# Two-layer hybrid decoder trunk on one core: paired 64-row scores, X^T by transposition, and moved steps where the mix and the MLP groups end

## What is computed

```python
h = rms_norm(x, ln_mix_pre)
(a_q, a_k, a_v, i_q, i_k, i_w, b_q, b_k, b_v, b_a, b_b, b_z,
 c_q, c_k, c_v, c_g, gate_logits) = split_projection(h @ w_in)
# A: scores = sum_h relu(iq_h . ik) * w_h; keep the 128 best causal keys of each query;
#    attention of 4 heads of 128 over them
# B: conv + SiLU on q/k/v, delta rule in chunks, T = inverse(I + M), gated
# C: retention, 4 heads with keys of 64, fixed decay, gated
merged = g0 * (y_a @ w_ba) + g1 * (y_b @ w_bb) + g2 * (y_c @ w_bc)
x = x + rms_norm(merged @ w_out, ln_mix_post)
ff = jnp.square(jax.nn.relu(rms_norm(x, ln_mlp_pre) @ w_up)) @ w_down
x = x + rms_norm(ff, ln_mlp_post)
```

## Time and profile before

| | |
|---|---|
| time of the runs | 1983.54 us median, 1982.48 to 1984.13 |
| profiled execution | 1989.03 us, span 1987.2 us |
| mean granted TensorE clock | 0.989 |
| busy share of the span | TensorE 97%, weight loads 78%, VectorE 58%, ScalarE 24%, POOL 18% |
| chain that ended last | TensorE 91%, ScalarE 4%, VectorE 3%, issue 2% |

### The profile page before, as it was taken

How to read it: one execution, slowest core, us unless ns; L and a number is a source line. 1 busy time by engine, 2 the same in 40 slices (tenths; PEclk the granted TensorE clock), 3 DMA queues, 4 the chain that set the end, 5 groups by cost and what they waited for, 6 DMA issues and landing times.

```text
span 1987.2 us, 25235 instructions
## 1 busy us (share of the span) xinstructions
PE 1932.3 (97%) x8926; PEld 1556.1 (78%) x8926; DVE 1145.5 (58%) x1958; ACT 470.2 (24%) x919; POOL 348.7 (18%) x549
## 2 busy tenths in 40 slices
PE   8999999999999999999999999999999999999998
PEld 7867667879878888788878667678888788887887
DVE  6855688854464642454477557888434655424534
ACT  3153343211333100011122533523122331000111
POOL 2211111110120222222112111111101102221220
PEclk9999999999999999999999999999999999999999
DMA  6432112321430422222222321222215213332221
GB/s 233 138 117 70 64 59 88 90 75 56 178 117 1 145 98 96 85 95 95 85 85 97 116 69 64 69 79 89 79 49 214 73 44 116 99 101 83 99 96 53
DMA packets 72478, 186.79 MB, mean 94 GB/s; under 512 B 18304, under 2 KB 30784, under 8 KB 71488
## 3 DMA queue, kind: packets, MB, share of 16 engines
q1 hardware_dynamic: 41328, 152.10, 22.7%
q10 hardware_dynamic: 31056, 33.38, 5.0%
HBM read 174.40 MB, written 11.06 MB: 93 GB/s over the span
## 4 chain that ended last, share of the span: by engine, by line
PE 91%; ACT 4%; DVE 3%; issue 2%; POOL 0%; DMA 0%; ACTq 0%; SPq 0%; POOLq 0%; DVEq 0%
PE psD L1043 23%; PE psD L1045 22%; PE psD L1044 22%; PE psM L1043 4%; PE psM L1045 4%; PE psM L1044 4%; PE psM L1102 2%; PE psM L1109 1%; PE psM L1305 1%; PE psM L1199 1%; PE psM L1207 1%; PE psM L1323 1%; PE psM L1311 1%; ACT wide L1543 1%; PE psM L1116 1%
## 5 line engine op out<-in xcount | busy, mean ns | idle before, releaser
L1043 PE MATMUL psD<-a_hi,w_hi 128*128 128x512 f32 (+2 forms) x1488 | 601.4, 404 | 14.2 <-DVE wide L2272 6.6
L1045 PE MATMUL psD<-a_hi,w_lo 128*128 128x512 f32 (+2 forms) x1488 | 578.9, 389 | 0.0
L1044 PE MATMUL psD<-a_lo,w_hi 128*128 128x512 f32 (+2 forms) x1488 | 578.3, 389 | 0.0
L953 DVE TENSOR_TENSOR w_lo<-raw,w_hi 128x1024 fp32r<-128x1024 f32 x208 | 255.4, 1230 | 306.5 <-POOL w_hi L1021 305.7
L1043 PEld LDWEIGHTS psD<-a_hi,w_hi 128*128 128x128 f32 (+1 forms) x1488 | 281.8, 189 | 96.0 <-issue 32.2
L1020 POOL TENSOR_TENSOR w_hi<-raw,tabs 128x1 fp32r<-128x1 f32 x272 | 60.8, 223 | 1599.8 <-PE psD L1045 1376.8
L1045 PEld LDWEIGHTS psD<-a_hi,w_lo 128*128 128x128 f32 (+1 forms) x1488 | 281.4, 189 | 58.9 <-issue 0.3
L1044 PEld LDWEIGHTS psD<-a_lo,w_hi 128*128 128x128 f32 (+1 forms) x1488 | 281.9, 189 | 58.2 <-issue 4.5
L1021 POOL TENSOR_SCALAR w_hi<-raw 128x1023 fp32r<-128x1023 f32 x272 | 296.8, 1091 | 0.0
L1801 ACT CAST f_hi<-gt 128x512 f32 x64 | 40.0, 624 | 487.4 <-DVE gt L2244 487.4
L2241 DVE TENSOR_SCALAR gt<-psD 128x512 f32<-128x512 f32 x64 | 44.3, 691 | 140.2 <-PE psD L1045 140.2
(11 more groups left out here) (269 smaller groups left out, 2620.2 us busy)
## 6 DMA issues: line engine op xcount, KB each, us to landing
raw<-in_ws SPq DMA_DIRECT2D x272, 512.0 KB, 3.3
s_raw<-in_wo ACTq DMA_DIRECT2D x14, 512.0 KB, 11.1
out<-x SPq DMA_DIRECT2D x8, 512.0 KB, 5.1
x<-rows_d ACTq DMA_DIRECT2D x4, 1024.0 KB, 5.7
x<-out ACTq DMA_DIRECT2D x2, 2048.0 KB, 8.4
e_raw<-in_wo ACTq DMA_DIRECT2D x8, 512.0 KB, 6.5
tabs<-in_tab SPq DMA_DIRECT2D x1, 2944.0 KB, 12.2
x<-in_x SPq DMA_DIRECT2D x4, 512.0 KB, 6.6
```

What stands on the lines that cost most here:

```text
L953: dve.tensor_tensor(w_lo[:, s, :], raw[:, s, :], w_hi[:, s, :].bitcast(F32), ALU.subtract) \
L1043: pe.matmul(out, lhi, rhi, start=start, stop=False)
L1044: pe.matmul(out, lhi, rlo, start=False, stop=False)
L1045: return pe.matmul(out, llo, rhi, start=False, stop=stop)
```

## The change

Seven edits, all in the lists of steps and in the steps themselves; the computation stays.
1. `rs(a, m)` and `index(tb, a)` issue two matmuls one behind the other, on partitions 0 to 63 and 64 to 127, into two banks. The steps on VectorE and ScalarE stay per head. In the planner, the ring of three banks becomes a choice of the banks that are free first. Retention takes two heads at a time, so the second head's output accumulates in one of the three small banks.
2. `xt` at levels 4 and 5 turns the new X; ScalarE copies it to X^T. Level 6 stays a product, subtracted on VectorE.
3. The probabilities are scaled on ScalarE, and the reciprocal stays on VectorE.
4. In the prefix `rot 4` comes behind the units 6 and 7. The w_lo of the planned region's second slab is issued with the prefix, not by the planner. The planner's starting times change.
5. In the tail the stays come earlier, each with a semaphore of its own for its load. `lo_merged` for 0 to 3 comes before merge 2's slab, for 4 and 5 before merge 3's. ScalarE's table load comes behind the last a_hi. The first token tile takes the staying slabs in another order.
6. x1 is turned among the slabs of the tiles 2 and 3, and the splits move with it.
7. At the end of a group the last `lo_slab` comes after `add_half1`.

```diff
+TURNS = {(2, 2): 0, (2, 5): 1, (3, 5): 2}
@@ schedule
     for r in range(4):
-        prefix.append(("rot", r + 1))
-        if r == 3:
+        if r < 3:
+            prefix.append(("rot", r + 1))
+        else:
             prefix += [("piece", j, "cv", 0) for j in range(PIECES - 1)] + [("cv", 0)]
         for j in (2 * r, 2 * r + 1):
             prefix.append(("unit", j))
...
+        if r == 3:
+            prefix.append(("rot", 4))
         prefix.append(("turn", r))
...
+    def paired(w):
+        return .207 + .213 * w
...
-            op("pe", "xt", n, l, t=.9, to=("dve", "XT", n, l), after=[("act", "left", n, l), ("dve", "XT", n, l - 1), ("pe", "xx", n, l)])
-            op("dve", "XT", n, l, t=read(2, 1.2), after=[("pe", "xt", n, l), ("dve", "X", n, l)])
+                op("pe", "xt", n, l, t=.44, to=("act", "XT", n, l), after=[("dve", "X", n, l)])
+                op("act", "XT", n, l, t=copied(), after=[("pe", "xt", n, l)])
+            else:
+                op("pe", "xt", n, l, t=.9, to=("dve", "XT", n, l), after=[("act", "left", n, l), ("act", "XT", n, l - 1)])
+                op("dve", "XT", n, l, t=read(2, 1.2), after=[("pe", "xt", n, l)])
...
-            op("dve", "prob", tb, h, t=.2 + read(w, slow), after=[("act", "sexp", tb, h), ("dve", "smax", tb, H - 1)])
+            op("dve", "rinv", tb, h, t=.2, after=[("act", "sexp", tb, h)])
+            op("act", "prob", tb, h, t=copied(w), after=[("dve", "rinv", tb, h)])
...
-    free = {"pe": 0.0, "act": 9.0, "dve": 11.0}
+    free = {"pe": 0.0, "act": 4.0, "dve": 5.0}
...
-    rounded(slabs + 2, 0.0)
-    first_slab = slabs_before = slabs + 1
+    first_slab = slabs_before = slabs + 2
...
+    def emptied(bank):
+        return end.get(user[bank], 1e9) if user[bank] else 0.0
+
+    def ring(n):
+        return sorted(range(3), key=emptied)[:len(drain[n])]
...
+        if n == ("pe", "vn", 0):
+            at = max(at, 2.5)
         if n in drain:
-            at = max(at, drained([drain[u] for u in small[-3:-2]]) + latency if len(small) >= 3 else 0)
+            at = max(at, emptied(ring(n)[-1]) + latency)
...
-    tail += [("mgate", "B", 3), ("merge", "B", 0), ("mgate", "B", 4), ("mgate", "B", 5), ("merge", "B", 1), stays[0],
-             ("mgate", "B", 6), stays[1], ("mgate", "B", 7), stays[2], ("merge", "B", 2), *stays[3:5], ("merge", "B", 3), *stays[5:]]
+    tail += [("mgate", "B", 3), ("merge", "B", 0), ("mgate", "B", 4), ("mgate", "B", 5), stays[0], ("merge", "B", 1), *stays[1:3],
+             ("mgate", "B", 6), *stays[3:5], ("mgate", "B", 7), *stays[5:], ("merge", "B", 2), ("merge", "B", 3)]
...
     opened = every(prefix, 0)
-    opened.remove(("dve", "lo", slabs_before + 1))
@@ TensorE
-                    def index(tb, i):
+                    def index(tb, a):
+
                         pe.wait_ge(*on("rot_done", 9))
-                        hp = slice(64 * (i % 2), 64 * (i % 2) + 64)
-                        ps = small_bank(("il", tb, i))
-                        small_done(pe.matmul(ps[:, 0:(tb + 1) * P], iq[hp, i // 2, cut(tb)],
-                                             ik[hp, 0:(tb + 1) * P], start=True, stop=True))
+                        banks = [small_bank(("il", tb, 2 * a + i)) for i in range(2)]
+                        for i, ps in enumerate(banks):
+                            hp = slice(64 * i, 64 * i + 64)
+                            small_done(pe.matmul(ps[:, 0:(tb + 1) * P], iq[hp, a, cut(tb)],
+                                                 ik[hp, 0:(tb + 1) * P], start=True, stop=True))
...
                     def xt(n, l):
-                        if l == FIRST:
-                            pe.wait_ge(*on(f"xi_in{n % 2}", 32 * (n // 2 + 1)))
-                        right("xt", n, l)
+                        if l == LEVELS - 1:
+                            right("xt", n, l)
+                        else:
+                            for s, v in drained(("xx", n, l)):
+                                pe.wait_ge(*on(s, v))
+                            turn_heads(("xt", n, l), lambda h: B["X", n % 2][:, cut(h)])
...
-                        for j, (_, k, ks, c, _) in enumerate(STAYING):
+                        for j in (0, 1, 3, 4, 5, 2, 6) if t == 0 else range(len(STAYING)):
+                            _, k, ks, c, _ = STAYING[j]
+                            if (t, j) in TURNS:
+                                turn_x1(TURNS[t, j])
...
-                    for t in range(READY):
+                    for t in range(ST):
                         out_tile(t)
-                    for t in range(READY - 1):
-                        turn_x1(t)
-                    out_tile(ST - 1)
-                    turn_x1(READY - 1)
@@ ScalarE
                     def left(n, l):
                         if l > FIRST:
-                            mid(act, ("xt", n, l - 1))
+                            mid(act, ("xx", n, l - 1))
...
+                    def turned(n, l):
+                        sig(act.copy(B["XT", n % 2], mid(act, ("xt", n, l))[:, :]), f"XT{n % 2}")
...
+                    def prob(tb, h):
+                        w = slice(0, (tb + 1) * P)
+                        act.wait_ge(*on("rinv", H * tb + h + 1))
+                        sig(act.activation(pr[:, h, w], pr[:, h, w], ACT.Copy, scale=rinv[:, h:h + 1]), "prob")
...
                     def stay(j):
-                        if j == 0:
-                            act.wait_ge(*on("stay_in", 16 * len(STAYING)))
+                        act.wait_ge(*on(f"stay_in{j}", 16))
...
                     slab(act, ("mgate", "B", KT - 1))
-                    act.preload_act_table_set("natural_log_exp_and_others")
                     for k in range(KT):
                         act.wait_ge(*on("merged", KT + k + 1))
                         sig(act.mul(a_hi[:, k, :], wt[:, k, :], 0.5), "a_hi")
+                    act.preload_act_table_set("natural_log_exp_and_others")
...
-                        if t == READY - 1:
-                            for i in range(READY - 1):
-                                hi_x1(i)
+                        for i in {1: (0, 1), 2: (2,)}.get(t, ()):
+                            hi_x1(i)
@@ VectorE
-                        if b and j == 3:
-
-                            for k in range(KT - 2):
+                        if b and j >= 2:
+
+                            for k in (range(4), range(4, 6))[j - 2]:
                                 lo_merged(k)
...
-                        if t == READY:
-                            lo_x1(READY - 1)
                         diagonal("pre_mlp", t)
-                        if t == READY - 1:
-                            for i in range(READY - 1):
-                                lo_x1(i)
+                        for i in {1: (0, 1), 2: (2,)}.get(t, ()):
+                            lo_x1(i)
...
                         add_half0(g)
-                        lo_down(g, range(FG // 2, FG))
+                        lo_down(g, range(FG // 2, FG - 1))
                         for t in range(ST):
                             add_half1(g, t)
+                        lo_down(g, [FG - 1])
```

More of the change, by code:

```diff
@@ L253, in schedule @@
     op("act", "cv", 3, t=ST * copied(), after=[("pe", "cv", 3)])
[L255 to L267, removed]
+    for i in range(ST * H // 2 + 1):
+        if i < ST * H // 2:
+            a, m = divmod(i, ST)
+            pair = range(2 * a, 2 * a + 2)
+            past = [("pe", "rv", 2 * ((i - 2) // ST) + 1, (i - 2) % ST)] if i >= 2 else []
+            op("pe", "rs", a, m, t=paired(ST - m), to=[("dve", "rp", h, m) for h in pair], after=[("act", "cv", 3)] + past)
+            for h in pair:
+                freed = ("pe", "rv", h, m - 1) if m else ("pe", "rv", h - 2, ST - 1)
+                op("dve", "rp", h, m, t=read(ST - m), after=[("pe", "rs", a, m), freed])
+        if i:
+            a, m = divmod(i - 1, ST)
+            for h in range(2 * a, 2 * a + 2):
+                op("pe", "rv", h, m, t=column(ST - m), to=("act", "ret", h) if h % 2 and m == 0 else None,
+                   after=[("dve", "rp", h, m), ("act", "cv", 3)])
+                if m == ST - 1:
+                    op("act", "ret", h, t=copied(), after=[("pe", "rv", h, m)])
     order = None
@@ L296, in schedule @@
                 ring = [("dve", "index", (q - 2) // IH + 1, (q - 2) % IH)] if q >= 2 else [("pe", "rv", H - 1, ST - 1)]
-                op("pe", "index", tb, i, t=column(w), to=("act", "index", tb, i), after=[("dve", "turn", 8)] + ring)
-                op("act", "index", tb, i, t=copied(w), after=[("pe", "index", tb, i)] + ring)
+                if i % 2 == 0:
+                    op("pe", "index", tb, i // 2, t=paired(w), to=[("act", "index", tb, i), ("act", "index", tb, i + 1)],
+                       after=[("dve", "turn", 8)] + ring)
+                op("act", "index", tb, i, t=copied(w), after=[("pe", "index", tb, i // 2)] + ring)
                 op("dve", "index", tb, i, t=read(w, slow) + (.3 if i == IH - 1 else 0),
```

(23 more changed lines are left out.)

62 lines of the change are left out of this document (28 added, 34 removed).

## The result

The changed kernel takes 1934.8 us (median of four executions, 1933.2 to 1942.1) against 1983.8 of the kernel before: a ratio of 0.9758, 95% interval 0.9742 to 0.9775, or 48 us less. The profiled execution took 1936.0 with a span of 1934.2, 53.0 less than the span of the profiled one before.

What follows compares the result with a forecast made beforehand. TensorE bounds the kernel, busy in 97% of the span, with its waits and low clock behind some. 16.5 + 7.4 + 9.1 + 6.8 + 8.9 + 11.3 - 6 = 54.0 off 1983.5 gives 1929.5 us, range 1918 to 1950.

Steps and rivals of the forecast that it cites:

- pairs: rs and index steps between dense matmuls: fewer 64-row detours on TensorE save 14.7 to 18.1 us, taken as 16.5.
- X^T: Levels 4 and 5: transposing instead of products saves 0.46 us on each of 16 steps, 7.4 us; dense pieces cover the chain.
- probabilities: Scaling moved to ScalarE: no gain taken, as TensorE never waits for the removed line; some 5 us possible loss.
- prefix: Waits for the last unit and a w_lo, plus low clock behind: 9.1 us gained, between 5 and 11.7.
- out slabs: Waits for a_lo going into the out slabs, plus clock: 6.8 us gained (4 to 8), w_lo then late by 0.65.
- x1: Turning among the out slabs lets the up slabs start 2.76 us earlier per layer; with clock 8.9, lower end 5.
- groups: Between the groups: TensorE's 3.3 us wait per layer and the low clock go, 11.3 us gained (10 to 12).
- new waits: Between 176 and 500, pairs ask for two small banks at once: three more waits per layer, 6 us lost.
- the list does not fit (1): Rival: slightly wrong planner durations cause many waits between 176 and 500; gain 20 to 32, time 1951 to 1963, chance 0.10.
- turning lowers the clock (2): Rival: clock falls to 1.2 GHz around each of 16 more turnings, costing 27 to 48: 1957 to 1978, chance 0.02.
- Pairs without overlap (3): Rival: the second matmul's bank is held until the first is over, losing all 16.5: 1946 us, chance 0.03.
- Waits of 1.5 us at each pair (4): Rival: TensorE waits for a second bank at all 40 detours; slower from 1.5 us each, 1997 at twice 0.93, chance 0.04.

Runs made afterwards that it cites:

- e5: Changed kernel with X^T at levels 4 and 5 computed again by four products and a subtraction on VectorE: 1935.4 us, ratio 0.9749.
- e12: The kernel of e11 with X^T at levels 4 and 5 by products and a subtraction on VectorE again: 1926.1 us, ratio 0.9709.
- e1: Changed kernel with the last w_lo of a group put back ahead of the four adds: 1948.7 us, ratio 0.9823.
- e2: Changed kernel with x1 turned behind the tiles again instead of among the slabs, splits included: 1942.3 us, ratio 0.9798.
- e3: Changed kernel with the old tail: late stays, one semaphore, old merge order, table load and first-tile order: 1943.9 us, ratio 0.9801.
- e6: Changed kernel with the old prefix end: rot 4 before the last units, later w_lo, old planner starting times: 1946.5 us, ratio 0.9816.
- e9: Changed kernel with its list of steps kept, but probabilities scaled on VectorE at the reciprocal's place: 1937.1 us, ratio 0.976.
- e11: Changed kernel with the joint table loaded before each fin following a tanh, and table changes (1.28 us) counted by the planner: 1924.4 us, ratio 0.9701.
- e10: Changed kernel with X^T by products and subtraction, and probabilities scaled, both on VectorE as before: 1947.2 us, ratio 0.9811.

## Why the prediction was right, and where it was not

The forecast was 1929.5, the time 1934.8; the gain 54.0 against 48 to 49, and between the two profiled spans 53.0. Part by part, in us (forecast; cost of undoing it alone):

| part | forecast | undone alone |
|---|---|---|
| pairs | 16.5 | 11.5 |
| X^T | 7.4 | -1.8 (by the traces 1 to 2, e5 and e12) |
| probabilities | 0 | 10.3 with a new list, 0.4 with the same |
| prefix | 9.1 | 11.5 |
| out slabs | 6.8 | 8.5 |
| x1 | 8.9 | 7.9 |
| groups | 11.3 | 12.9 |
| new waits | -6 | in the rows above |

Split by kind, the forecast had 23.9 of TensorE's instructions, 16.2 of waits and 13.9 of clock. The two profiled spans show 25.5, 15.7 and 11.8.

**The seams held.** Prefix, out slabs, x1 and groups were forecast at 36.1 and measure 40.8. They have a fixed place in the program, and each wait could be followed from its row to its cause. Their clock did not come back as forecast: 6.8 us in the traces of e1, e2, e3 and e6 together, for 13.9 in the sum. That the medians agree as well as they do is in part luck. The late next was named rightly: w_lo ahead of the first out slab, 1.12 instead of the 0.65 forecast, and the 0.72 ahead of the last up columns, which stayed.

**The planned stretch did not come apart as I had it.** Its sum was right: 16.5 + 7.4 - 6 = 17.9. From unit 7 to the last fin step the first layer is 16.3 us shorter (511.5 - 130.8 before, 494.4 - 130.0 after) and the second 13.2 (1495.6 - 1118.6 and 1451.7 - 1087.8). Of these 29.5 the prefix's own waits are 7.4 and the low clock behind them 4.1, which leaves 18. But the terms were not right. The instructions did get cheaper as costed, 13.2 for the pairs (forecast 16.5, lower bound 14.7) and 7.0 for X^T (7.4). The step that failed is that this time is a gain. There the planner makes a new list for every edit, and part of TensorE's work removed comes back as waits: 4.5 with the pairs, 4.8 with X^T. "Dense pieces lie between these steps and cover it" holds for most of the 16 steps and not for the one at 382, behind the scalings. And "I take nothing" for the probabilities was wrong by 10, since that edit changes the list for the better. That the misses of pairs and X^T and the gain of the probabilities cancel is luck. The parts undone one by one add to 60.8, with the probabilities at 0.4 to 50.9, near the 48 of the whole.

**The new waits were of the right size by another cause.** I took three more per layer; from 176 to 515 the waits of the first layer go from 4.2 to 7.6. But none of them stands in front of a pair, and the largest, 2.63, is ScalarE's tables.

**The level was taken wrongly.** Between the two profiled spans the gain was 53.0, and the forecast 54.0. The step that failed is the last one: "I take the gains from the median, and expect a profile of the changed kernel to lie as much above its own." The profile of before lay 5.5 above its median, that of after 1.2, and that is 4.3 of the 5.3 by which the forecast was too low. The sum had 13.9 us of clock in it (4.3, 1.5, 3.4 and 4.7), all from one execution; between the profiled executions the clock gave 21.3 - 9.5 = 11.8. Of the kernel before, the nine executions beside e9 read 0.993 at 1982.3 us and 0.989 at 1989.3: a fall that is in the profile is not in every execution, and the median has fewer. The forecast also left out a fall that its own trace has, 3.0 us from 266 to 276. And its low end, 1950, takes 13 us for new waits where its own bound is 15; it should have been 1952.

**The rivals.** That the list does not fit (1) was in part so, as e11, with other loads and another list, is 10 us below; its 1951 to 1963 was far too much. That turning lowers the clock (2) fell: 16 falls would be 27 us or more, and the changed kernel's two falls cost 6.8 and stand at none of the new turnings. With the turning undone (e5) the executions have clocks of 0.995 to 0.998, against 0.992 to 0.997, and the same time. Pairs without overlap (3) fell with the 1.13 of the row at 313.48. Waits of 1.5 us at each pair (4) fell: there is none at any of the 40. Of the signs named, the 20 visits per layer with four records, the clock and the 16 us less of waiting came out; the wait at the first out slab stayed just above 1 us.

## What to carry to other kernels

Where a seam has a fixed place, follow its wait to the cause, name what is late next, and the gain can be told to some 2 us. Where a list scheduler sets the order, a cheaper instruction is worth what the new list makes of it: cost both the engine that gains the work in that very stretch and what the planner leaves out (here a table load of 1.28 us), and test an edit once with the list kept. How many falls of the clock there are differs from one execution of a kernel to the next: take them from one near the median, or count a part of them.

## What the runs showed of the hardware

**The same short wait sometimes costs seven times itself.** In both layers of the changed kernel TensorE waits 0.7 us for a_lo ahead of the last up columns, with rows alike up to there. The stretches, first layer and then second:

```profile
618.00:622.00 4.00, 3.27 (x26) 1.00 0.02 4
622.00:626.00 4.00, 4.00 (x36) 1.00 0.21 49
...
1576.00:1580.00 4.00, 3.27 (x27) 1.00 0.00 0
1580.00:1584.00 4.00, 4.00 (x30) 0.75 0.40 111
1584.00:1588.00 4.00, 4.00 (x18) 0.50 0.83 316
1588.00:1592.00 4.00, 4.00 (x11) 0.50 1.01 385
```

After the same 0.73 the clock is at 1.2 GHz for some ten microseconds in the second layer, 5 us lost, and not in the first. Of the 26 such waits in the profiles of the changed kernel and its twelve variants, 7 are followed by a fall of this size (one of them in the first layer, in e10). In e11 it is so in the profiled execution (1930.6 us, clock 0.994), and three others of its five took 1923.8 to 1924.4 at 0.999. Longer waits are no surer: behind the 3.3 us at a group's end the clock fell in both layers of the kernel before, in e1 only in the second, and behind the 2.93 for a_lo in the first layer of the kernel before and in neither of e3. The Trainium skill, "TensorE: Matmul & The Clock Gate", HAM oscillation, ties such falls to idle gaps of the engine that repeat with each group of matmuls. Here a single one of 0.73 us is followed by a fall in some profiles and by none in others. What decides between the two stays open, and no run took this wait away.

**Two matmuls on different halves of the rows cost one.** 1.13 us for four records of 512 columns at all 12 pairs of that width in the changed kernel, against 1.12 for two records in the earlier trace rows.
